# Where wide operands and their weights stand within 256 bytes, in a two-block transformer kernel on one core

## The reference, cut to what matters

```python
proj = h @ w_in                          # block 1, "in1": 43 column tiles of 128, with 16 meta tokens: 272 rows
m    = y @ w_out                         # block 1, "out1": 16 column tiles, 260 rows
g    = causal_dwconv(rms(h) @ w_gate)    # block 1, "gu", even tiles: 44 tiles, 260 rows (a halo of 4)
u    = rms(h) @ w_up                     # block 1, "gu", odd tiles: 44 tiles, 256 rows
f    = (silu(g) * u) @ w_down            # block 1, "down"
...                                      # block 2: in2, up projections, ba/bb, out2, wq
s    = rms(h) @ u_emb.T ; out = coef @ v_emb   # the expert layer, "U" and "V", 128 tiles each
```

## Time and profile before

| | |
|---|---|
| runs | 3317.62, 3318.67, 3318.78 us; median 3318.67 |
| profiled execution | 3317.44 us; its span 3315.7 us, 1.7 us less |
| TensorE busy | 3282.1 us, 99% of the span |
| VectorE, ScalarE, GpSimd busy | 2173.4, 1675.5, 102.7 us |
| moved by DMA | 593.11 MB, 179 GB/s |

### The profile page before, as it was taken

How to read it: one execution, slowest core, us unless ns; L and a number is a source line. 1 busy time by engine, 2 the same in 40 slices (tenths; PEclk the granted TensorE clock), 3 DMA queues, 4 the chain that set the end, 5 groups by cost and what they waited for, 6 DMA issues and landing times.

```text
span 3315.7 us, 60045 instructions
## 1 busy us (share of the span) xinstructions
PE 3282.1 (99%) x24732; PEld 3111.5 (94%) x24732; DVE 2173.4 (66%) x3665; ACT 1675.5 (51%) x2626; POOL 102.7 (3%) x136
## 2 busy tenths in 40 slices
PE   8999999999999999999999999999999999999998
PEld 8998999999999999899999999999999998888887
DVE  8875476666665476565666798878755555556655
ACT  5465454444444455445455444666544444445544
POOL 0000200000000000000000000122100000000000
PEclk9999999999999999999999999999999999999999
DMA  6443545555566655344565555544455555566554
GB/s 210 148 134 128 170 158 190 186 184 184 185 190 193 194 168 178 124 147 163 187 195 193 199 195 195 175 150 151 163 192 192 191 192 194 193 207 219 190 188 159
DMA packets 165439, 593.11 MB, mean 179 GB/s; under 512 B 18608, under 2 KB 19248, under 8 KB 165040
## 3 DMA queue, kind: packets, MB, share of 16 engines
q1 hardware_dynamic: 165168, 589.27, 54.1%
HBM read 585.00 MB, written 4.19 MB: 178 GB/s over the span
## 4 chain that ended last, share of the span: by engine, by line
PE 98%; DVE 1%; ACT 0%; DMA 0%; issue 0%; SPq 0%; ACTq 0%
PE ps L822 31%; PE ps L823 31%; PE ps L824 30%; PE ps L1308 2%; PE ps L875 0%; PE ps L1109 0%; DVE wl L1380 0%; PE ps L1081 0%; PE ps L858 0%; PE ps L1136 0%; PE ps L877 0%; PE ps L1135 0%; PE ps L878 0%; PE ps L1146 0%; PE ps L1131 0%; PE ps L1322 0%
## 5 line engine op out<-in xcount | busy, mean ns | idle before, releaser
L2140 ACT CAST wh<-raw 128x1024 fp32r<-128x1024 f32 (+2 forms) x1116 | 1159.1, 1039 | 1262.7 <-PE ps L824 1262.3
L1380 DVE TENSOR_TENSOR wl<-raw,wh 128x1024 fp32r<-128x1024 f32 (+2 forms) x1116 | 1347.1, 1208 | 500.7 <-ACT wh L2140 497.6
L822 PE MATMUL ps<-xh,wh 128*128 128x256 f32 (+2 forms) x5184 | 1469.1, 283 | 19.8 <-DVE xl L1388 10.2
L823 PE MATMUL ps<-xl,wh 128*128 128x256 f32 (+2 forms) x5184 | 1449.9, 280 | 0.0
L824 PE MATMUL ps<-xh,wl 128*128 128x256 f32 (+2 forms) x5184 | 1446.0, 279 | 0.0
L822 PEld LDWEIGHTS ps<-xh,wh 128*128 128x128 f32 x5184 | 977.3, 189 | 26.3 <-issue 11.4
L823 PEld LDWEIGHTS ps<-xl,wh 128*128 128x128 f32 x5184 | 977.4, 189 | 2.2
L824 PEld LDWEIGHTS ps<-xh,wl 128*128 128x128 f32 x5184 | 978.4, 189 | 0.0
L823 PE MATMUL ps<-wl,ch 128*128 128x512 f32 x1024 | 401.1, 392 | 0.0
L824 PE MATMUL ps<-wh,cl 128*128 128x512 f32 x1024 | 400.3, 391 | 0.0
L822 PE MATMUL ps<-wh,ch 128*128 128x512 f32 x1024 | 400.2, 391 | 0.0
(11 more groups left out here) (385 smaller groups left out, 3157.5 us busy)
## 6 DMA issues: line engine op xcount, KB each, us to landing
raw<-in_peer_u SPq DMA_DIRECT2D x256, 512.0 KB, 4.3
raw<-in_peer_v SPq DMA_DIRECT2D x256, 512.0 KB, 4.4
raw<-in_w_in SPq DMA_DIRECT2D x186, 512.0 KB, 3.7
raw<-in_w_up SPq DMA_DIRECT2D x82, 512.0 KB, 4.2
raw<-in_w_gate SPq DMA_DIRECT2D x80, 512.0 KB, 4.2
raw<-in_w_down SPq DMA_DIRECT2D x80, 512.0 KB, 4.1
raw<-in_w_out SPq DMA_DIRECT2D x64, 512.0 KB, 3.9
raw<-in_w_branch_a SPq DMA_DIRECT2D x16, 512.0 KB, 3.5
```

What stands on the lines that cost most here:

```text
L822: t.matmul(o, lh, rh, start=start, stop=False)
L823: t.matmul(o, lh, rl, start=False, stop=False)
L1380: v.tensor_tensor(part_at(wl, i), raw_at(i), part_at(wh, i).bitcast(F32), ALU.subtract).then_inc(lo, 1)
L2140: s.copy(part_at(wh, i), raw_at(i)).then_inc(hi, 1)
```

## The change

Rows of x for the first block's norms, and rows of y, become 320 words (1,280 bytes, 5 × 256) long, so all of them have one place within 256. The longer rows don't fit into xh and xl alone: `xw` covers both (16 high rows and 11 low ones), and the last 5 low rows go to a further tile, `x1_end` or `x2_end`. The blocks of wide weights go back from a pitch of 144 words to 128, so all blocks of a chunk have one place too, and `shift` moves whole chunks: by 16 bytes times the tile's number, modulo 16 instead of 4. Odd gu tiles and guk chunks aren't shifted. The pads change so that in1, out1 and the odd gu tiles have x at place 16, the even ones at 0. The cast and the subtraction of a wide chunk write 1,024 columns in one piece, where they wrote eight pieces of 128.

```diff
-PAD_X, PAD_Y, PAD_A, PAD_C = (44, 24, 28, 28), 12, 44, 28
+PAD_X, PAD_E, PAD_Y, PAD_A, PAD_C = (28, 24, 28, 28), (44, 48), 44, 44, 28
+XROW = 320
+TAIL = 11
-WIDE = ("in1", "out1", "gu")
-WROW = 144
...
-    return 4 * (m % 4) if name != "gu" else 0 if m % 2 else 4 * (m // 2 % 4)
+    return 4 * (m % 16) if name in ("in1", "out1") else 4 * (m // 2 % 16) if name == "gu" and m % 2 == 0 else 0
...
-    wh = alloc(top, "wh", [128, SN, 8 * WROW], F32R)
-    wl = alloc(top, "wl", [128, SN, 8 * WROW], F32R)
-    xbuf = [alloc(top, f"x{i}", [128, KT * (T1 + 4)], F32R) for i in "hl"]
+    wh = alloc(top, "wh", [128, SN, CH + 128], F32R)
+    wl = alloc(top, "wl", [128, SN, CH + 128], F32R)
+    x_wide = ExitStack()
+    xw = alloc(x_wide, "xw", [128, 8832], F32R)
+    x_wide.close()
+    xbuf = [alloc(top, f"x{i}", [128, 4416], F32R) for i in "hl"]
...
-    yh, yl = [alloc(mixed_scope, f"y{i}", [128, 64 + 16 * T1], F32R)[:, PAD_Y:PAD_Y + 16 * T1].rearrange(
-        "p (k t) -> p k t", t=T1)[:, :, 0:TQ] for i in "hl"]
+    yh, yl = [alloc(mixed_scope, f"y{i}", [128, 64 + 16 * XROW], F32R)[:, PAD_Y:PAD_Y + 16 * XROW].rearrange(
+        "p (k t) -> p k t", t=XROW)[:, :, 0:TQ] for i in "hl"]
+    x_end = [alloc(mix, "x1_end", [128, PAD_E[0] + (KT - TAIL) * XROW], F32R)]
...
+    x_end.append(alloc(wide, "x2_end", [128, PAD_E[1] + (KT - TAIL) * XROW], F32R))
...
+    def normed_at(half, norm, k, c0, n):
+        if norm >= 2:
+            o = PAD_X[norm] + S * k + c0
+            return xbuf[half][:, o:o + n]
+        if half and k >= TAIL:
+            o = PAD_E[norm] + XROW * (k - TAIL) + c0
+            return x_end[norm][:, o:o + n]
+        o = PAD_X[norm] + XROW * (KT * half + k) + c0
+        return xw[:, o:o + n]
...
     def row_at(w, i, r):
-        o = WROW * r + shift(i) if PLAN[i][0] in WIDE else 128 * r
+        o = 128 * r + shift(i)
         return w[:, i % SN, o:o + 128]
     def part_at(w, i):
-        if PLAN[i][0] in WIDE:
-            o = shift(i)
-            return w[:, i % SN, :].rearrange("p (r c) -> p r c", c=WROW)[:, :, o:o + 128]
-        o = key_row(i)
-        return w[:, i % SN, o:o + cols(i)]
-    def key_row(i):
-        name, k, _ = PLAN[i]
-        return 16 * (k % 4) if name == "guk" else 0
+        return w[:, i % SN, shift(i):shift(i) + cols(i)]
```

More of the change, by code:

```diff
@@ L524, in build @@
     u_t = alloc(ffn, "u_t", [128, 2, S])
+    wide = ExitStack()
+    x_end.append(alloc(wide, "x2_end", [128, PAD_E[1] + (KT - TAIL) * XROW], F32R))
+    wide.close()
     wide = ExitStack()
@@ L617, in build @@
     cmean = tmp[:, 4, 0:TQ]
-    def normed_at(half, norm):
-        t = T1 if norm < 2 else S
-        return xbuf[half][:, PAD_X[norm]:PAD_X[norm] + KT * t].rearrange("p (k t) -> p k t", t=t)
+    def normed_at(half, norm, k, c0, n):
[7 more added lines that the diff above has]
+        return xw[:, o:o + n]
     def row_at(w, i, r):
-        o = WROW * r + shift(i) if PLAN[i][0] in WIDE else 128 * r
+        o = 128 * r + shift(i)
         return w[:, i % SN, o:o + 128]
     def part_at(w, i):
-        if PLAN[i][0] in WIDE:
-            o = shift(i)
-            return w[:, i % SN, :].rearrange("p (r c) -> p r c", c=WROW)[:, :, o:o + 128]
-        o = key_row(i)
-        return w[:, i % SN, o:o + cols(i)]
-    def key_row(i):
-        name, k, _ = PLAN[i]
-        return 16 * (k % 4) if name == "guk" else 0
-    def raw_at(i):
-        x = raw[:, i % RN, 0:cols(i)]
-        return x.rearrange("p (r c) -> p r c", c=128) if PLAN[i][0] in WIDE else x
+        return w[:, i % SN, shift(i):shift(i) + cols(i)]
     def pc(name, i=0):
@@ L839, in halves @@
         def halves(norm, T, c0=0):
-            h, l = normed_at(0, norm), normed_at(1, norm)
-            return lambda k: (h[:, k, c0:c0 + T], l[:, k, c0:c0 + T])
+            return lambda k: (normed_at(0, norm, k, c0, T), normed_at(1, norm, k, c0, T))
         def pair(i0, outs, rhs, norm):
@@ L1014, in by_rows @@
                 for n in range(ROWS):
-                    c = slice(key_row(i0 + k) + 128 * n, key_row(i0 + k) + 128 * n + 128)
-                    last = three(outs[n], wh[:, (i0 + k) % SN, c], wl[:, (i0 + k) % SN, c], *rhs[n % 2](k), k == 0, k == KT - 1)
+                    last = three(outs[n], row_at(wh, i0 + k, n), row_at(wl, i0 + k, n), *rhs[n % 2](k), k == 0, k == KT - 1)
                 last.then_inc(gemm, 1)
@@ L1379, in cut @@
             v.wait_ge(hi, i + 1)
-            v.tensor_tensor(part_at(wl, i), raw_at(i), part_at(wh, i).bitcast(F32), ALU.subtract).then_inc(lo, 1)
+            v.tensor_tensor(part_at(wl, i), raw[:, i % RN, 0:cols(i)], part_at(wh, i).bitcast(F32), ALU.subtract).then_inc(lo, 1)
         def whole(i):
@@ L1387, in low_row @@
             v.wait_ge(xhi, 16 * norm + k + 1)
-            v.scalar_tensor_tensor(normed_at(1, norm)[:, k, 0:T], ht[:, k, c0:c0 + T], pc(gain_name, k),
-                                   normed_at(0, norm)[:, k, 0:T].bitcast(F32), ALU.mult, ALU.subtract).then_inc(xlo, 1)
+            v.scalar_tensor_tensor(normed_at(1, norm, k, 0, T), ht[:, k, c0:c0 + T], pc(gain_name, k),
+                                   normed_at(0, norm, k, 0, T).bitcast(F32), ALU.mult, ALU.subtract).then_inc(xlo, 1)
         def sum_rows(norm, rows, T, part):
@@ L2139, in cut @@
                 s.wait_ge(gemm, i - SN + 1)
-            s.copy(part_at(wh, i), raw_at(i)).then_inc(hi, 1)
+            s.copy(part_at(wh, i), raw[:, i % RN, 0:cols(i)]).then_inc(hi, 1)
         def whole(i):
@@ L2145, in high_row @@
         def high_row(norm, k, c0, T, gain_name):
-            s.activation(normed_at(0, norm)[:, k, 0:T], ht[:, k, c0:c0 + T], ACT.Copy, scale=pc(gain_name, k)).then_inc(xhi, 1)
+            s.activation(normed_at(0, norm, k, 0, T), ht[:, k, c0:c0 + T], ACT.Copy, scale=pc(gain_name, k)).then_inc(xhi, 1)
         def squares_of(sq_, c0, T, i):
```

## The result

The changed kernel takes 3311.12 us (median of 16 runs, 3310.43 to 3312.40), the kernel before 3318.68 (16 runs, 3317.24 to 3320.53): 7.6 us less, a ratio of 0.9977 with an interval of 0.9970 to 0.9985. A second profile and 11 more runs of the same kernel gave 3311.52, ratio 0.9977 (0.9968 to 0.9986). I had forecast 19.1 us. The direction and the range hold, the size does not: the time is that of rival C, 3310.5.

A forecast was written before the change was run, and what follows sets the result against it. TensorE, busy 99% of the span, was taken as the bound, so time is a sum of matmul start distances. Odd gu tiles' 8.2 us plus wide tiles' 10.9 gave 19.1 us off 3318.7: 3299.6 us, range 3285 to 3314.

The forecast's parts named there:

- rival C: Only odd gu tiles gain; matmuls of 260 and 272 columns stay as they are: 3310.5 us, chance 0.24.
- Odd gu tiles: 41 tiles, 1,968 matmuls, reach down's 113.3 ns from 118.3: 9.8 us less 1.6 for entry, gain 8.2 us.
- Even gu tiles, in1 and out1: Wide matmuls of 260 and 272 columns: half of the sixteen places taken as fast, gain 10.9 us.
- The floor: Estimated shortest matmul distance at 0.443 ns a column: 115.1 ns for 260 columns, 120.4 for 272.
- nothing: Lower bound for even gu tiles, in1 and out1: a gain of 0, since holding a place doesn't itself make it fast.
- The 21.8 us above: Upper bound if all even gu, in1 and out1 matmuls ran at the floor: 9.2 + 8.9 + 3.7 us.
- guk, cast, subtraction, DMA: guk gains 0, at most 1.7 us; cast and subtraction change nothing, hidden by TensorE; DMA loads keep up.
- Rival F: DVE in in1 becomes the bound, or V turns slow at 2800, on top of rival C: about 3316, chance 0.05.
- V: right as 0: Side effect on V's speed, from 5.7 us shorter after 3100 to 8.7 us longer from 2800: expected value 0.
- B: Every held place is fast, whatever the number of columns: 3288.7 us, chance 0.14.
- E: Slower kernel: bad relations of x and w are held for 48 matmuls; 3331 us at 9 ns, chance 0.06.
- D: Places play no part; odd gu tiles are slow from neighbours or the cast's writes: 3318.7 us, chance 0.09.

The follow-up runs named there:

- one-operand runs: Changed kernel with odd gu weights stepping again, x held: 3319.14 us; kernel before with odd gu weights held, x stepping: 3318.67 us.
- map of 260 columns: Changed kernel with each of U's 256 chunks moving 260 columns at its own pair of x and weight places: 3363.48 us.
- run of widths: Changed kernel with U's first 48 tiles moving 256 to 512 columns, four tiles per width, at held places: 3400.59 us.

## Why the prediction was wrong in size

**Odd gu tiles: right.** 8.2 us forecast, (5.679 − 5.481) × 41 = 8.1 measured, entry cost included. The one-operand runs show that both operands have to be held. But the step as such is only half of the cause. Down's run at sixteen places shows that thirteen of them, held, cost 116.7 to 120.0 ns, and stepping costs 118.3. The odd tiles gained because they were put at x 16 and w 160, the pair that rows of down and U had shown as fast.

**Even gu tiles, in1 and out1: the step that failed.** It is this term of the sum: "I take half of the sixteen places as fast, since the rows of held places show both: 10.9 us." Measured: 0.2 us from even gu tiles, about 0.1 from out1, −0.9 from in1, so −0.6 in all. Two things in it were wrong. The floor, 115.1 and 120.4 ns, was a scale drawn through rows of other N, and no chunk of any run reaches it. The prediction's own sign of failure, that N of 260 or 272 can't be held fast at all, is what these runs show. And "half" was a guess at how often a place is fast. For 260 columns the sixteen pairs of even gu average 119.9 ns, held or stepping; even for 256, where fast pairs exist, only one to three of the sixteen places make one. Svw at 125 ns with 272 columns held was the nearest row, of the right N, and said so; I gave it 0.24 and let uk and V, rows of other N, set the term. The total of 3311.12 us lies inside the stated range only because the range reaches up to rival C.

**The bounds.** Below, "nothing" was nearly met. The 21.8 us above were out of reach of every value measured here: at the shortest distances seen in whole chunks, 118.3 for 260 columns (out1) and 123.1 for 272, the gain would be (1,920 + 768) × (119.9 − 118.3) + 2,064 × (124.7 − 123.1) = 7.6 us. The run with one good pair per stage got only part of that, 2.3 us under the changed kernel, mostly because in1 doesn't keep its fast pattern.

**guk, cast, subtraction, DMA: right.** Per k guk went from 2.50 to 2.51 us, 0.2 us in all, so it gained nothing. TensorE's waits are 19.6 us in sum against 19.3; the 0.3 is a new one, for `x_end`. The subtraction in gu takes the same time as before:

```profile
L1378 DVE TENSOR_TENSOR wl<-raw,wh x162: 1212/1218/1227, 478.9 to 929.3; 128x1024 fp32r<-128x1024 f32 x162
```

Rival F, DVE as the bound, is out.

**V: right as 0, and the reason holds.** Its pattern after 3100 is the slow one before and after; a change of place shows that it is a matter of how V returns after its coefficients came late.

**The other rivals.** B, every place fast, and E, held slow, are both out: held places average what stepping gave. D is out: the odd tiles alone don't say it, since the change altered the writes too, but down lost its speed by the place of its weights alone, and with the short writes gone and x stepping the odd tiles stayed at 5.694 us. C was right in the time, and in its reason.

**The page's rule.** The same 256-column matmul at the same granted clock of 1.00 and with no step takes 113.3 to 120.4 ns by the pair of places. The Trainium skill, TensorE: Matmul & The Clock Gate, Part 2's step-by-step (step 1), says that loading the next weights takes no bandwidth from the running matmul. I had read it as "places don't matter"; the measurement decides against that reading. Whether the two reads get in each other's way isn't shown. Why one pair is fast and another isn't was not settled. In the map of 260 columns 204 of 256 values are within 0.35 ns of the one with both places 32 bytes further on, and with x alone moved 86 are; so the places seem to count against each other, and an interplay of the two reads suggests itself. That is argued, not shown.

## What to carry to other kernels

Read the distance between matmul starts, per tile, at the N and the layout in question; a floor carried over from another N is worth nothing here. Holding both operands of a matmul at one place within 256 bytes pays only at a pair measured as fast for that N; at another it can cost as much as stepping, or more. So scan pairs, one per tile, in one run and take the best. Then test it in the real stage, since a pair can hold a fast and a slow pattern and a scan sees one of them: prefer one that comes back after an interruption, as V's 240 did.

## What the runs showed of the hardware

- With a new weight block for every matmul, 256 held columns cost 113.3 to 120.4 ns by the pair of places, 260 cost 118.3 to 123.7, 272 cost 123.0 to 127.2, and 512 cost 226.7 to 233.5.
- In the run of widths at x 16 and w 160 the distance is N + 16 cycles of 2.4 GHz for 256 columns, N + 32 for 272, 288, 320, 352 and 384, and neither for the rest.
- One pair can hold two patterns: 272 columns at x 16, w 160 ran at 126.7 ns in one run and at 123.1 in another, and at x 16, w 96 at 123.3 and 126.7 within one stage.
- At unchanged places V runs at 227 ns until its coefficients come late, near 3086 us, and at 233.4 from then or a few chunks later on; with its second half at 240 it returns to 227.
- After the pause between out1 and gu, the clock granted over the same 7.6 us was 0.79 in one profile and 0.55 in another, worth about 1.3 us (guk's first two chunks, 7.81 us against 6.50).
